# Expert rows: gather the kept, unscaled rows and apply rstd through a diagonal while a chunk is turned

## What is computed

```python
h = rmsnorm(x, norm_ffn[l])          # x * rsqrt(mean(x*x) + eps) * gain
grp = argmax(softmax(h @ w_group + b_group))             # one group of 8
top_p, top_i = top_k(softmax(e_logits of that group), 2) # two experts of 64
order = argsort(flat_e)                                  # 1024 rows sorted by expert
xs = x_pad[slot_tok]                                     # gathered rows of h
ys = (silu(xb @ w_gate[e]) * (xb @ w_up[e])) @ w_down[e] # per block and expert
```

## Time and profile before

| | us |
|---|---|
| median of 3 runs | 1646.93 (1641.90 to 1648.56) |
| the profiled execution, its own time | 1643.47 |
| its span in the profile | 1641.7 |
| PE busy | 1443.8 (88%) |
| PEld busy | 901.5 (55%) |
| DVE busy | 605.2 (37%) |
| ACT busy | 340.4 (21%) |
| POOL busy | 244.4 (15%) |
| DMA engines, mean | 293 GB/s |

### The profile page before, as it was taken

How to read it: one execution, slowest core, us unless ns; L and a number is a source line. 1 busy time by engine, 2 the same in 40 slices (tenths; PEclk the granted TensorE clock), 3 DMA queues, 4 the chain that set the end, 5 groups by cost and what they waited for, 6 DMA issues and landing times.

```text
span 1641.7 us, 24136 instructions
## 1 busy us (share of the span) xinstructions
PE 1443.8 (88%) x8971; PEld 901.5 (55%) x8971; DVE 605.2 (37%) x1517; ACT 340.4 (21%) x983; POOL 244.4 (15%) x290
## 2 busy tenths in 40 slices
PE   8999999999899987878778899999899977878775
PEld 3655466655466655545555455755566655545453
DVE  2145577742532222222223447423522222222225
ACT  2122367741110000000001335512100000000000
POOL 1122100000211111111112133000211111111112
PEclk9999999999999999999999999999999999999998
DMA  7115030036599999999999401472899999999997
GB/s 294 44 52 218 39 155 1 2 142 230 226 351 427 429 430 428 431 428 431 428 429 419 158 1 52 205 293 105 324 385 428 429 429 428 429 429 429 431 429 294
DMA packets 44373, 480.67 MB, mean 293 GB/s; under 512 B 11034, under 2 KB 11562, under 8 KB 24656
## 3 DMA queue, kind: packets, MB, share of 16 engines
q1 hardware_dynamic: 28144, 450.17, 65.5%
q0 software_dynamic: 15008, 25.37, 4.4%
q10 hardware_dynamic: 1152, 4.19, 0.6%
HBM read 461.33 MB, written 47.19 MB: 310 GB/s over the span
## 4 chain that ended last, share of the span: by engine, by line
PE 57%; DMA 33%; DVE 6%; issue 2%; ACT 1%; POOL 0%; DVEq 0%; SPq 0%
DMA sb_arena<-moe_w 32%; PE ps L1164 12%; PE ps L1358 7%; PE ps L1573 7%; PE ps L1173 6%; PE ps L1679 2%; PE ps L1709 2%; PE ps L1694 2%; PE ps L1539 2%; PE ps L1399 2%; PE ps L1427 2%; PE ps L1423 1%; PE ps L1510 1%; PE ps L1260 1%; PE ps L1607 1%
## 5 line engine op out<-in xcount | busy, mean ns | idle before, releaser
L1164 PE MATMUL ps<-sb_arena,sb_x_block 128*64 128x256 f32 x4096 | 476.9, 386 | 96.6 <-DMA sb_arena<-moe_w 89.0
L1164 PEld LDWEIGHTS ps<-sb_arena,sb_x_block 128*64 128x64 f32 x4096 | 419.9, 197 | 205.8 <-issue 134.7
L1173 PE MATMUL ps<-sb_arena,sb_hidden_space 128*64 128x512 f32 x1024 | 248.0, 605 | 44.0 <-ACT sb_hidden_space L894 43.3
L768 POOL DMA_INDIRECT expert_rows<-sb_y_sb,sb_row_now x124 | 132.3, 1067 | 751.3 <-DVE sb_y_sb L1945 687.5
L1944 DVE COPY sb_row_now<-sb_row_of 128x1 uint32 (+1 forms) x124 | 19.0, 154 | 600.2 <-PE ps L1173 583.5
L894 ACT COPY sb_hidden_space<-ps 128x128 f32<-128x128 f32 x128 | 34.0, 265 | 756.2 <-PE ps L1239 750.7
L1173 PEld LDWEIGHTS ps<-sb_arena,sb_hidden_space 128*64 128x64 f32 x1024 | 62.1, 136 | 141.1 <-issue 74.2
L1358 PE MATMUL ps<-sb_sorted_rows,sb_arena 128*128 128x512 f32 x256 | 114.6, 594 | 2.1 <-DVE sb_arena L2184 1.3
L1955 DVE TENSOR_TENSOR sb_x_block<-sb_sorted_rows,sb_moe_gain 128x512 f32<-128x512 f32 x124 | 85.9, 692 | 25.0 <-issue 20.7
L1945 DVE COPY sb_y_sb<-ps 128x512 f32<-128x512 f32 x124 | 84.4, 681 | 0.0
L1358 PEld LDWEIGHTS ps<-sb_sorted_rows,sb_arena 128*128 128x128 f32 x256 | 46.9, 190 | 51.4 <-issue 48.8
(11 more groups left out here) (309 smaller groups left out, 1492.6 us busy)
## 6 DMA issues: line engine op xcount, KB each, us to landing
sb_arena<-moe_w SPq DMA_DIRECT2D x116, 3072.0 KB, 38.1
sb_arena<-moe_w SPq DMA_DIRECT2D x10, 2048.0 KB, 9.0
sb_arena<-moe_w SPq DMA_DIRECT2D x16, 1024.0 KB, 6.7
sb_sorted_rows<-nsa_w_group SPq DMA_DIRECT2D x2, 2048.0 KB, 13.2
sb_arena<-nsa_w_group SPq DMA_DIRECT2D x2, 2048.0 KB, 7.9
sb_sorted_rows<-nsa_w_out SPq DMA_DIRECT2D x1, 4096.0 KB, 12.1
kept_rows<-sb_arena SPq DMA_DIRECT2D x8, 512.0 KB, 4.6
token_rows<-sb_arena ACTq DMA_DIRECT2D x8, 512.0 KB, 2.7
```

What stands on the lines that cost most here:

```text
L768: pool.indirect_dma_start(out=ys_dram.rearrange("r (j n) -> (r j) n", j=2), out_offset=bass.IndirectOffsetOnAxis(ap=row_now[:, u:u + 1], a ...
L1164: last = nc.tensor.matmul(ps[j * BLOCK:(j + 1) * BLOCK, bank, 0:2 * P].rearrange("p (g n) -> p g n", g=2), x_rows[:, :, k], weights[:, 0:2 ...
L1173: last = nc.tensor.matmul(ps[j * BLOCK:(j + 1) * BLOCK, 2, :], hidT[:, c * BLOCK:(c + 1) * BLOCK], weights[:, 2, c * D + j * 512:c * D + ( ...
```

## The change

Raw rows are gathered, from `kept_rows`; `token_rows` and the scaled copies are gone. The eps-normalised factor of each token follows the routing: POOL splits rstd of all tokens into three bfloat16 parts, DVE multiplies the chunk one-hot table by them, PE inverts that table with eight more small matmuls (24 columns instead of 8), and DVE adds the three parts to `sorted_rstd`, one number for each sorted row. ACT writes a diagonal 128 x 128 matrix for each chunk. `turn_chunk` then is a plain float32 matmul of the slice with that diagonal where it was a transpose against the identity. Token numbers go through the inversion less 256, in bfloat16. The one-hot tables move from chunk 0's place to chunk 7's. SP no longer waits for `token_rows`: it waits for the squares, the turned halves, the logits and the kept rows.

```diff
-        low_hot = sorted_space[:, 0:4 * P].bitcast(F16)...
-        high_hot = sorted_space[:, 8 * P:8 * P + 32].bitcast(F16)...
+        hot_space = xs_in(CHUNKS - 1)
+        low_hot = hot_space[:, 0:4 * P].bitcast(BF16)...
...
@@ moe_loads (SP)
-                    if t == 1:
-                        sp.wait_ge(first_rows_sent, 32 * (l + 1))
+                    if t == 2:
+                        sp.wait_ge(ssq_ready, squared(2 * l + 1, 1))
+                        sp.wait_ge(h_turned, 2 * (TILES * 2 * l + 1) + 2)
                         part(RING + 1, RING + 1, 0, 1).then_inc(weights_loaded[RING + 1], 16)
-                sp.wait_ge(last_rows_sent, 32 * (l + 1))
                 sp.wait_ge(logits_done, TILES * (l + 1))
                 part(RING + 2, RING + 2, 1, 3).then_inc(weights_loaded[RING + 2], 16)
+                sp.wait_ge(x_kept, 16 * TILES * (l + 1))
+                sp.wait_ge(ssq_ready, squared(2 * l + 1, TILES - 1))
                 part(RING + 1, RING + 1, 1, 2).then_inc(weights_loaded[RING + 1], 16)
@@ moe_moves (POOL)
-                pool.wait_ge(token_ready, l + 1)
-                pool.wait_ge(first_rows_sent, 32 * (l + 1))
-                pool.wait_ge(last_rows_sent, 32 * (l + 1))
+                pool.wait_ge(x_kept, 16 * TILES * (l + 1))
+                pool.wait_ge(token_ready, 2 * l + 1)
                 for c in range(CHUNKS):
+                    if c == CHUNKS - 1:
+                        pool.wait_ge(token_ready, 2 * l + 2)
                     pool.indirect_dma_start(
-                        out=xs_in(c), out_offset=None, in_=h_dram,
+                        out=xs_in(c), out_offset=None, in_=x_dram,
@@ norm_scales (POOL), after the last tile's rstd
+                    step(pool.tensor_copy(rstd_part[:, 0], both(rstd[:, :])))
+                    step(pool.tensor_tensor(rstd_rest[:, :], rstd[:, :], rstd_part[:, 0, 0, :], ALU.subtract))
+                    step(pool.tensor_copy(rstd_part[:, 1], both(rstd_rest[:, :])))
+                    step(pool.tensor_tensor(rstd_rest[:, :], rstd_rest[:, :], rstd_part[:, 1, 0, :], ALU.subtract))
+                    pool.tensor_copy(rstd_part[:, 2], both(rstd_rest[:, :])).then_inc(rstd_split, 1)
@@ norm_squares (ACT)
-                    def send(t):
...
-                        nc.scalar.activation(x[:, t, :], x[:, t, :], ACT.Copy, scale=rstd[:, t:t + 1]).then_inc(h_ready, 1)
-                        act.wait_ge(h_ready, TILES * layer + t + 1)
-                        act.dma_start(h_dram[t * P:(t + 1) * P, :], x[:, t, :])...
@@ moe_act (ACT)
+                def row_scales(chunks):
+                    for c in chunks:
+                        nc.scalar.activation(rstd_diag_of(c), ident, ACT.Copy, scale=sorted_rstd[:, c:c + 1]).then_inc(diag_ready, 1)
...
+                act.wait_ge(token_ready, 2 * l + 2)
+                row_scales(range(CHUNKS // 2))
                 chunk_half(0)
                 chunk_half(1)
+                act.wait_ge(tables_ready, l + 1)
+                row_scales(range(CHUNKS // 2, CHUNKS))
                 gate(base, 0)
@@ moe_pe (PE)
-                    last = nc.tensor.matmul(ps[:, 0, 0:CHUNKS], low_hot[:, c, :], high_hot[:, c, :],
+                    last = nc.tensor.matmul(ps[:, 0, 0:CHUNKS], low_hot[:, c, :], token_hot[:, c, :],
...
-                keep_busy(6)
+                pe.wait_ge(hots_ready, 2 * l + 2)
+                for c in range(TOPK * TILES):
+                    last = nc.tensor.matmul(ps[:, 2, 0:3 * CHUNKS].rearrange("p (r n) -> p r n", r=3), low_hot[:, c, :],
+                                            rstd_hot[:, :, c, :], start=(c == 0), stop=(c == TOPK * TILES - 1))
+                last.then_inc(inverted, 1)
+                keep_busy(3)
@@ turn_chunk (PE)
+                    pe.wait_ge(diag_ready, l * CHUNKS + c + 1)
...
-                            last = nc.tensor.transpose(
+                            last = nc.tensor.matmul(
                                 ps[:, CHUNK_BANK + 2 * (c % 2) + half, :].rearrange("p (n k) -> p k n", k=KD)[:, k, :],
-                                xs_in(c)[part].rearrange("p (m k) -> p k m", k=KD)[:, k, :], ident[part, part])
+                                xs_in(c)[part].rearrange("p (m k) -> p k m", k=KD)[:, k, :], rstd_diag_of(c)[part, part],
+                                start=True, stop=True)
@@ route (DVE)
+                dve.wait_ge(rstd_split, l + 1)
+                v.tensor_tensor(rstd_hot, chunk_hot.unsqueeze(1)..., rstd_part..., ALU.mult).then_inc(hots_ready, 1)
...
-                v.tensor_copy(token_of[:, :], ps[:, 0, 0:CHUNKS]).then_inc(token_ready, 1)
+                v.tensor_scalar(token_of[:, :], ps[:, 0, 0:CHUNKS], float(S // 2), None, ALU.add).then_inc(token_ready, 1)
+                dve.wait_ge(inverted, 2 * l + 2)
+                v.tensor_reduce(sorted_rstd[:, :], ps[:, 2, 0:3 * CHUNKS].rearrange("p (r n) -> p n r", r=3), AX, ALU.add
+                                ).then_inc(token_ready, 1)
```

More of the change, by code:

```diff
@@ L801, in norm_scales, with both @@
                     pool.tensor_tensor(rstd[:, t:t + 1], rstd[:, t:t + 1], minus_half[:, 0:1], ALU.pow).then_inc(rstd_ready, 1)
+                if n % 2 == 0:
+                    def both(one):
+                        return one.unsqueeze(1).to_broadcast([P, TOPK, TILES])
+                    pool.wait_ge(rstd_ready, TILES * n)
+                    step(pool.tensor_copy(rstd_part[:, 0], both(rstd[:, :])))
[3 more added lines that the diff above has]
+                    pool.tensor_copy(rstd_part[:, 2], both(rstd_rest[:, :])).then_inc(rstd_split, 1)
             for ph in range(PHASES):
@@ L858, in turn_copy @@
                     turned_half(m, t)
-                if layer is not None:
-                    def send(t):
-                        act.wait_ge(rstd_ready, n * TILES + t + 1)
-                        act.wait_ge(x_kept, 16 * (TILES * layer + t + 1))
-                        act.wait_ge(h_turned, 2 * (TILES * m + t) + 2)
-                        nc.scalar.activation(x[:, t, :], x[:, t, :], ACT.Copy, scale=rstd[:, t:t + 1]).then_inc(h_ready, 1)
-                        act.wait_ge(h_ready, TILES * layer + t + 1)
-                        act.dma_start(h_dram[t * P:(t + 1) * P, :], x[:, t, :]).then_inc(
-                            first_rows_sent if t < 2 else last_rows_sent, 16)
-                    for t in range(TILES):
-                        turn_copy(t)
-                        if t >= 1:
-                            send(t - 1)
-                        square(t)
-                    send(TILES - 1)
-                    return
                 for t in range(TILES):
```

35 lines of the change are left out of this document (22 added, 13 removed).

## The result

The changed kernel takes 1690.72 us (median, 1688.74 to 1691.05) against 1645.35 us before (1641.90 to 1648.56): a ratio of 1.0275, with a 95% interval of 1.0255 to 1.0295. The profiled execution takes 1691.05 us, its span is 1689.3 us, 47.6 more than the span before. The forecast was 1676, a loss of 30 us where 45 were measured; the measured time lies inside the stated range, near its upper end. Lines are those of the changed kernel where it is read: `turn_chunk` L1280, expert products L1178 and L1187, hidden turn L1258.

The account below looks back on a forecast made before the run. Weight streams bound each MoE, their end set by PE's opening. Start, clock and six chunks gave +14.8 us a layer (0.8 - 1.9 + 15.9; 1.4 - 2.5 + 15.9), +29.6 on 1646.9: 1676.5 us, range 1651 to 1694.

Parts of the forecast that it names:

- What bounds the kernel: Each MoE's end moves one for one with the end of expert 4, set by PE's work in the opening.
- Turning as a matmul: In turn_chunk, 16 passes at 0.226 us make a chunk 3.6 us, 2.65 us more than with transposes.
- Six chunks: Chunks 2 to 7, turned between the up products of experts 0 to 2, uncovered: +15.9 us a layer.
- L1164's step: Weight loads at L1164 with a step of eight floats, reported at 197 ns, not 136; taken as the turning's pace.
- columns alone: Rival 1: a turning load costs its columns alone, 1.9 us a chunk; time 1651, chance 0.12.
- Gathers: In the opening, first rows land 1.8 us earlier in layer 0 and 1.2 in layer 1.
- the bound that I had set aside as the lower one: First product's start set by PE turning both chunks ahead: 445.3 against 446.2 us in layer 0.
- The clock: Turning matmuls ahead of the first product bring full clock there: -1.9 us in layer 0, -2.5 in layer 1.
- Hidden work: POOL's split, second inversion, sum of parts, diagonals and the last gather's wait are covered and cost nothing.
- rival 3: Slow clock holds through the opening, chunks' matmuls cost about twice: about +9 us a layer, 1695; chance 0.07.
- The faster case: Rival 2: turning stays nearly free and the opening starts sooner; 1634 us, chance 0.04.
- start: Start of expert 0's first product, waiting for block 0: +0.8 us in layer 0, +1.4 in layer 1.

Follow-up runs that it names:

- the run with six idle matmuls: The changed kernel with six idle matmuls behind the inversions in place of three; 1690.73 us, ratio 1.0286.
- the run side by side: The changed kernel with each slice's 128 stationary columns read side by side, not at a step of eight floats; 1662.53 us, ratio 1.0109.
- The run with transposes: The changed kernel with chunks turned by transposes against the identity, scaling by rstd left out; 1643.28 us, ratio 0.9991.
- rows scaled with idle matmuls: The changed kernel with transposes, landed rows scaled by ACT (half of chunk 0 by DVE), POOL's two waits exchanged and more idle matmuls; 1645.08 us, ratio 1.0035.
- held gathers with idle matmuls: The kernel before with three idle matmuls added and POOL's gathers of chunks 2 to 7 held until chunk 0 is turned; 1641.4 us, ratio 1.0017.

## Why the prediction was right, and where its size was off

- **What bounds the kernel**: right. Loss in the opening and shift of the end agree to 0.2 us of 48, and expert 2's to the last expert's product takes what it did.
- **Turning as a matmul**: right in mechanism, and what it adds to a chunk 12% too small, 2.65 us where 2.97 were measured. I had 0.226 us a pass and loads reported at 310 ns; they are reported at 331, a pass takes 0.247, a chunk 3.95 and not 3.6. Six chunks cost +17.8 a layer, not +15.9. Halves go side by side, as said. Taking L1164's step for the price was what carried the forecast; columns alone would have given 1651.
- **Gathers**: wrong. I had them landing 1.8 and 1.2 us earlier, since the weights ahead of them would be through. The weights were through: the DMA engines are at share 0.29 from 434 to 438. But the first chunk still reached PE 5.8 us after POOL's issue (6.0 before) and 4.5 in layer 1 (5.2), so most of that time isn't the queue. And the issue itself came 0.85 us later, behind two waits. Chunk 0's turn began 0.6 and 0.1 us later than before, counted from the inversion. With PE then holding 7.9 us of turning ahead of the product, the first product came +2.8 and +3.7, not +0.8 and +1.4: the bound that I had set aside as the lower one, PE itself, was the one that held.
- **The clock**: wrong in sign. I had -1.9 and -2.5, and +2.7 and +2.9 were measured. The first product kept its half clock (+0.3 and 0), and I hadn't thought of the later stretches at all: in the course of each group of turning matmuls the granted clock fell again, so that it was halved for 37.5 us in each layer's opening (439.3 to 452.9, 459.8 to 470.0 and 476.8 to 490.5 in layer 0), where it had been 6.8. Those later stretches cost 2.4 and 2.9 us. I took "PE busy ahead" for what gives the clock; the run with six idle matmuls shows that this isn't enough, the run with full-width work in place of the later turning shows that the clock came back and stayed, and so does the run side by side, where the turning takes half as long.
- **Hidden work**: right. The run with transposes has all of it, at ratio 0.9991.
- **Rivals**: the slow clock (rival 3) was priced on a wrong ground: the chunks' matmuls don't slow down with the clock, since a load with the step takes 330 ns at full clock (454.3 to 458 us) and 332 at half (462.4 to 466.2). At half clock the products slow down (1.94 to 3.68 us for the down product), and so do loads side by side. The faster case needed a chunk under 1.5 us; even side by side it is 1.9.

- **The range**: it held by luck. The forecast's own width ended at 1688, below the measured 1690.7; only rival 3, with its wrong price, carried the range to 1694. Three terms of the sum missed in the same direction, the clock's by the most.

Sum of the misses a layer: turning +2, start +2.0 and +2.3, clock +4.6 and +5.3. With the forecast's 14.8 that is the 23.4 and 24.4 of the table.

## What to carry to other kernels

A plain float32 matmul in place of a float32 transpose has two passes for one, and with few moving columns its weight load is its price: read how the stationary operand lies in memory before its column count. When an operation on the critical path becomes longer, read also the products behind it, since a long run of matmuls like these turning ones can leave them a halved clock. Where a per-row factor has to be applied, an engine with time left beside PE's products did it for 0.2% of the kernel's time.

## What the runs showed of the hardware

- A float32 load of 128 stationary columns from 64 rows is reported at 188 ns side by side, 193 at a step of two floats, 325 at four, 331 at eight, at full clock; at half clock 327 side by side and 331 at eight.
- The page "TensorE: Matmul & The Clock Gate" of the Trainium skill, section "LDWEIGHTS (loading the stationary operand)", prices a load by columns: at full clock the trace agrees up to a step of two floats, and not beyond.
- PE's rows were without a gap from 454.3 us on, and the granted clock fell to 1.2 GHz at 459.8 all the same; what ran before it were 64-row, 64-column matmuls with 331 ns loads. Matmuls of the same shape with 188 ns loads, in stretches half as long, left it at 2.4 GHz (chunks 2 to 4 in 5.9 us, where the changed kernel has 12.0).
- The signal of chunk 0 came 1.0 to 4.7 us behind the modelled end of its last matmul in most openings with gathers under way or just issued, and within 0.1 us of it where they were held back or the last had been issued 4 us before. Two kernels had a chunk's signal on time with gathers under way (rows scaled with idle matmuls, chunk 0; held gathers with idle matmuls, chunk 1), so the cause stays open. Shown is only that holding the gathers back removed the delay for chunk 0, and that without idle matmuls the first product's signal then came late.
- POOL's first indirect gather was used by PE 4.4 us or more after its issue, even where the DMA engines were mostly idle (share 0.29 from 434 to 438 us in the changed kernel, first use 5.8 us after the issue).
